# Attention heads: alternating score halves, one operand for the sample rows, merged mask and rotation operations

## The chip, the core and the metric

The kernel runs on one NeuronCore of a Trainium2 chip as a single program. The metric is its device time in microseconds (us); of several runs the median is taken. The core's engines run side by side and meet at semaphores: TensorE (PE, matmuls, with its weight loads shown as PEld), VectorE (DVE), ScalarE (ACT), GpSimd (POOL), and SyncE (SP), which issues DMA transfers. Each engine works through its own instruction list in the order in which it is written; an instruction that waits for a semaphore holds up what stands behind it on that engine.

## The reference, cut to what matters

One inference step of a two-layer decoder trunk: layer 0 is an mLSTM mixer, layer 1 a differential-attention mixer. There are 1024 prompt tokens (`SEQ`) and 8 sample sequences of 4 tokens, 32 sample rows in all (`TS`). The change touches the attention over the prompt, with 8 heads (`H_B`), two components c of 64 columns each per head, and values of 128 columns:

```
p = rmsnorm(x, g) @ w_kv
k = rope(p[..., :QK_B].reshape(bsz, t_, H_B, 2, DK_B), pos)
v = p[..., QK_B:].reshape(bsz, t_, H_B, DV_B)
...
s = jnp.einsum('bqhcd,bkhcd->bhcqk', q, kp).astype(F32) * ATTN_SCALE
s = jnp.where(mk, s, -jnp.inf)
p = jax.nn.softmax(jnp.concatenate(scores, axis=-1), axis=-1)
w = p[:, :, 0] - lam * p[:, :, 1]
o = jnp.einsum('bhqk,bkhe->bqhe', w, vp)
...
rope: concatenate([x1 * cos - x2 * sin, x2 * cos + x1 * sin])
```

So every query block of 128 tokens needs, for each component c, a score product against all earlier keys, a causal mask on its last 128 columns, a row maximum, an exponential and a row sum; the two exponentials are then combined with one coefficient per row and multiplied with V. The head outputs go through an RMSNorm, a SiLU gate and an output projection.

## The kernel before, in words

The program is a row of phases: input norm, gates, mLSTM for the prompt, mLSTM for the samples, an output stage, `attention_phase`, the paged decode attention of the samples, and a second output stage. Only `attention_phase` is changed (and the constant table that it reads; the decode phase reads its mask from a smaller table with another offset).

Float32 operands are split into a high part and a low part (names ending in H and L, such as XH and XL for the normed input, WH and WL for the weights), and a product is three matmuls: high by high, high by low, low by high. TensorE has 8 PSUM banks `BK[0]` to `BK[7]`. `BK[4]` to `BK[7]` are the tensors PD: two banks for the scores of component 0, two for component 1.

`heads` runs the 8 heads: `sweep1` of head 0, then a hardware loop over 7 heads with `sweep2(h)` followed by `sweep1(h + 1)`, then the last `sweep2` and a tail.

`sweep1` takes 9 blocks t of 128 tokens (t = 8, written t == NT, is the block of the 32 sample rows). TensorE projects Q and K (`project`, 8 contraction tiles by 3 products, 24 matmuls), VectorE applies the rotation (`rotate`, five operations, L1786 to L1799), TensorE transposes the result (L1969), and ScalarE and VectorE cut it into high and low parts QTH, KTH (L1684, L1685) and QTL, KTL (L1840, L1841). Between these, ScalarE and VectorE cut the next weights (L1639, L1764).

`sweep2` takes the query blocks t = 0 to 7. I call the time from the first score matmul of t to that of t + 1 step t. TensorE's order in step t is: `scores(h, t)` (L1914), `turn_weights(h, t - 1)` (transposes of the combined weights, L1925, into `BK[2]` and `BK[3]`), `project_values(t + 1)` (24 matmuls, L1899, into the single bank B_V), `turn_output(h, t - 2)` (L1945) and `weigh(h, t - 1)` (the product with V, L1937). `scores` issues component 0 completely and then component 1; component c contracts over partitions 64c to 64c + 63 (a 64-row operand). For t = 4 to 7 a component has six matmuls (two column chunks of at most 512), for t = 0 to 3 three.

VectorE's order in step t is, for component 0: mask (L1860), row maximum (L1862), scaling (L1863); for t > 4 the copy of the upper transposed weights out of `BK[3]` (`weights`, L1820); `output(h, t - 2)` (L1813, after GpSimd's root, L1725 to L1727); then mask, maximum and scaling for component 1; `o_transposed(h, t - 3)` (L1806), for which `turn_output` of the next block waits; `sigmoid` (L1848); the cut of the next head's weights (L1764); and then, after both exponentials, the coefficients (L1877 to L1879) and the combination of the two exponentials (L1880), for which `turn_weights` waits.

ScalarE's order in step t is: `values` (three reads of B_V, L1652 to L1654, which free it for the next `project_values`), `weights(h, t - 1)` (the copy of the lower transposed weights out of `BK[2]`, L1668), the two exponentials (L1702), two weight cuts (L1639) and `squares` (L1661).

## Time and profile before

| what | value |
|---|---|
| median of 3 runs | 2052.78 us (2051.82 to 2057.74) |
| the profiled execution | 2055.39 us |
| its span, first to last instruction | 2053.7 us |
| TensorE, weight loads busy | 1813.7 us, 1618.6 us |
| VectorE, ScalarE, GpSimd busy | 1150.5 us, 810.9 us, 378.3 us |
| mean granted TensorE clock | 0.928 of full speed |
| first matmul of the attention phase | 943.6 us after the span's start |

Busy time is the time in which an engine had an instruction of the program in it. Matmuls are pipelined: each record is longer than the distance to the next one, so start times say how fast TensorE goes. Idle time in front of an instruction is put down to what ended it.

### The profile page before, as it was taken

The page shows a single profiled execution, that of the slowest core. Times are in us where ns is not written, and L with a number is a line of the kernel's source. Part 1 is how long each engine was busy: PE and PEld are TensorE (multiplying, and loading weights), DVE is VectorE, ACT ScalarE, POOL GpSimd, SP SyncE. Part 2 cuts the span into 40 slices and gives each one's busy share as a digit, 9 for nine tenths or more (in the row PEclk, how much of TensorE's full clock was granted, in tenths as well). Part 3 has the DMA queues.
Part 4 walks back from the last instruction along what each step waited for, and adds up shares of the span by engine and source line. Part 5 has one row for each costly group of instructions (what it writes and reads, how often), then busy time and mean ns, then how long its engine had stood idle before and what let it go on. Part 6 is the DMA issues. An engine that isn't in the chain of part 4 may idle for free. (4 is left out here: it accounts for less than half of the span.)

```text
span 2053.7 us, 38516 instructions
## 1 busy us (share of the span) xinstructions
PE 1813.7 (88%) x12115; PEld 1618.6 (79%) x12115; DVE 1150.5 (56%) x3272; ACT 810.9 (39%) x2237; POOL 378.3 (18%) x823
## 2 busy tenths in 40 slices
PE   5399999999999687897999999999999778888698
PEld 4399999999999665687889898888989766666376
DVE  4443543543543444345767676676767556666553
ACT  5333333333333222233535444354443346665522
POOL 1021221221221212011213122131221201111101
PEclk8699999999999866898999999999999979898799
DMA  4213123113111023332121111211110067676532
GB/s 119 65 32 66 8 57 65 10 55 65 10 56 15 24 81 82 135 119 68 42 54 33 31 33 38 57 33 31 33 31 23 21 217 272 237 275 235 176 101 106
DMA packets 149133, 165.10 MB, mean 80 GB/s; under 512 B 12762, under 2 KB 118074, under 8 KB 149042
## 3 DMA queue, kind: packets, MB, share of 16 engines
q1 hardware_dynamic: 144738, 159.85, 26.2%
q0 software_dynamic: 1184, 4.23, 0.8%
q8 instruction: 32, 0.52, 0.1%
q10 hardware_dynamic: 3120, 0.01, 0.1%
q14 instruction: 59, 0.48, 0.1%
HBM read 138.69 MB, written 25.37 MB: 80 GB/s over the span
## 5 line engine op out<-in xcount | busy, mean ns | idle before, releaser
L809 PE MATMUL PS<-WH,XH 128*128 128x384 f32 (+3 forms) x1152 | 369.2, 320 | 2.1 <-DVE WORK L731 2.1
L809 PE MATMUL PS<-WL,XH 128*128 128x384 f32 (+3 forms) x1152 | 356.8, 310 | 0.0
L809 PE MATMUL PS<-WH,XL 128*128 128x384 f32 (+3 forms) x1152 | 356.4, 309 | 0.0
L809 PEld LDWEIGHTS PS<-WH,XH 128*128 128x128 f32 (+1 forms) x1152 | 207.9, 180 | 7.0 <-DVE WORK L731 2.6
L809 PEld LDWEIGHTS PS<-WL,XH 128*128 128x128 f32 (+1 forms) x1152 | 208.0, 181 | 4.1
L809 PEld LDWEIGHTS PS<-WH,XL 128*128 128x128 f32 (+1 forms) x1152 | 207.6, 180 | 4.6
L1899 PE MATMUL PS<-WH,XH 128*128 128x256 f32 (+1 forms) x576 | 173.3, 301 | 2.3 <-ACT WORK L1654 2.1
L1899 PE MATMUL PD<-WH,XH 128*128 128x256 f32 (+1 forms) x576 | 169.4, 294 | 2.8 <-PEq L142 2.8
L1899 PE MATMUL PS<-WL,XH 128*128 128x256 f32 (+1 forms) x576 | 167.0, 290 | 0.0
L1899 PE MATMUL PS<-WH,XL 128*128 128x256 f32 (+1 forms) x576 | 166.5, 289 | 0.0
L1899 PE MATMUL PD<-WL,XH 128*128 128x256 f32 (+1 forms) x576 | 163.9, 285 | 0.0
L1899 PE MATMUL PD<-WH,XL 128*128 128x256 f32 (+1 forms) x576 | 163.5, 284 | 0.0
L1702 ACT ACTIVATE WORK<-PD,WORK 128x256 f32<-128x256 f32 (+7 forms) x128 | 95.0, 742 | 80.6 <-DVE WORK L1863 79.9
L2326 PE MATMUL PS<-cst,RAW 128*128 128x128 f32 x512 | 86.2, 319 | 41.2 <-DVE XL L2233 35.6
L2326 PEld LDWEIGHTS PS<-cst,RAW 128*128 128x128 f32 x512 | 67.6, 163 | 59.2 <-DVE XL L2233 43.2
L1899 PEld LDWEIGHTS PS<-WH,XH 128*128 128x128 f32 (+1 forms) x576 | 108.5, 188 | 4.9 <-ACT WORK L1654 3.9
L1899 PEld LDWEIGHTS PS<-WH,XL 128*128 128x128 f32 (+1 forms) x576 | 108.6, 188 | 0.7
L1899 PEld LDWEIGHTS PS<-WL,XH 128*128 128x128 f32 (+1 forms) x576 | 108.4, 188 | 0.6
L1899 PEld LDWEIGHTS PD<-WH,XH 128*128 128x128 f32 (+1 forms) x576 | 105.3, 183 | 3.3 <-issue 2.9
L1899 PEld LDWEIGHTS PD<-WH,XL 128*128 128x128 f32 (+1 forms) x576 | 105.3, 183 | 0.5
L1899 PEld LDWEIGHTS PD<-WL,XH 128*128 128x128 f32 (+1 forms) x576 | 105.1, 182 | 0.5
L2233 DVE TENSOR_TENSOR XL<-PS,XH 128x512 fp32r<-128x512 f32 x128 | 83.9, 685 | 38.5 <-ACT XH L2154 38.3
(354 smaller groups left out, 4301.3 us busy)
## 6 DMA issues: line engine op xcount, KB each, us to landing
RAW<-in_cache_k SPq DMA_DIRECT2D x64, 512.0 KB, 4.6
WORK<-in_cache_v SPq DMA_DIRECT2D x64, 512.0 KB, 4.4
RAW<-in_w_in_a SPq DMA_DIRECT2D x40, 512.0 KB, 6.3
RAW<-in_w_in_b SPq DMA_DIRECT2D x16, 512.0 KB, 5.4
RAW<-in_w_kv SPq DMA_DIRECT2D x16, 512.0 KB, 5.4
out<-WORK SPq DMA_DIRECT2D x16, 512.0 KB, 3.1
WORK<-in_x_prompt SPq DMA_DIRECT2D x8, 512.0 KB, 4.4
WORK<-d_G SPq DMA_DIRECT2D x8, 512.0 KB
```

Of the source, the lines that this page charges most:

```text
L809: last = nc.tensor.matmul(bank[0:rows, 0:n], x[:, k, tt], reg(w)[:, k, :], start=(i == 0), stop=(i == 3 * KT - 1))
L1702: act.activation(PR[:, c, 0:(t + 1) * P], S[c][:, 0:(t + 1) * P], ACT.Exp, scale=ATTN_SCALE, bias=nm[:, c:c + 1], accum_out=sm[:, c:c + 1] ...
L1899: last = nc.tensor.matmul(bank[0:rows, 0:N], x[:, k, tt], reg(w, r)[:, k, :], start=(i == 0), stop=(i == 3 * KT - 1))
L2233: v.tensor_tensor(XL[cols], BK[j].rearrange("p (h t) -> p h t", h=4), XH[cols].bitcast(F32), ALU.subtract).then_inc(kl, 1)
L2326: x = nc.tensor.transpose(BK[j][:, h * P:(h + 1) * P], KB[:, p % 4, (4 * j + h) * P:(4 * j + h + 1) * P], ident)
```

## The change

There are five edits, all in `attention_phase`.

1. `scores` issues the matmuls of the two components alternately (c = 0, 1, 0, 1, ...), with one wait for both exponentials of the block before and one semaphore count at the end, where it had one wait and one count for each component.
2. `project_values(t + 1)` is split for t = 1 to 6: its first 12 matmuls now stand ahead of `turn_weights(h, t - 1)`, the other 12 behind it.
3. The 32 sample rows of XH and XL are laid side by side once into a 64-column operand XS, so that a sample projection takes 16 matmuls in place of 24. The halves of the result stand on partitions 0 to 31 and 32 to 63; ScalarE copies the upper half (`sample_low`) and VectorE adds it to the lower one.
4. VectorE masks both components with one operation over both pairs of banks, then does the two maxima; `output(h, t - 2)` moves behind the second maximum. One reciprocal of both row sums and a copy stand in the place of two reciprocals.
5. `rotate` has three operations of 256 columns in place of one of 256 and four of 128: the sine table holds its sign, and one operand is read with its 32-column halves swapped.

```
-C_MS = C_SIN + NB * HALF
+C_MS = C_SIN + NB * DK
...
-        c[:, C_SIN + t * HALF:C_SIN + (t + 1) * HALF] = np.sin(ang)
+        c[:, C_SIN + t * DK:C_SIN + t * DK + HALF] = -np.sin(ang)
+        c[:, C_SIN + t * DK + HALF:C_SIN + (t + 1) * DK] = np.sin(ang)
...
-        PD = [ctx.enter_context(nc.psum_tensor(f"PD{k}", [P, 2, 512], F32)) for k in range(2)]
+        PQ = ctx.enter_context(nc.psum_tensor("PD", [P, 4, 512], F32))
+        PD = [PQ[:, 0:2, :], PQ[:, 2:4, :]]
...
+            XS = phase_tensor("XS", [P, KT, 2 * TS], F32R)
...
+            SB = PQ[:, :, :].rearrange("p (c a) n -> p c (a n)", c=2)
+            SPARE = YX[:, KT * TOK:KT * TOK + 6 * P].rearrange("p (a c) -> p a c", a=6)
+            SM, TL = SPARE[:, 0:4, :], SPARE[:, 4:6, :]
...
+                    act.activation(XS[:, :, 0:TS], XH[:, :, SEQ:TOK].bitcast(F32), ACT.Copy)
+                    act.activation(XS[:, :, TS:2 * TS], XL[:, :, SEQ:TOK].bitcast(F32), ACT.Copy).then_inc(xs_set, 1)
                     act.wait_ge(lamS, 1)
                     act.activation(le, mx, ACT.Exp).then_inc(lamE, 1)
+                    def sample_low(bank, turn):
+                        act.wait_ge(smd, turn)
+                        act.activation(TL[0:TS, :, :], bank[TS:2 * TS, 0:N].rearrange("p (a c) -> p a c", a=2), ACT.Copy)\
+                           .then_inc(tlow, 1)
...
-                            act.activation(SM[0:TS, 2:4, :], B_V[0:TS, 0:2 * P].rearrange("p (a c) -> p a c", a=2),
-                                           ACT.Copy).then_inc(smd, 1)
+                            sample_low(B_V, 2 * h + 1)
...
+                            if t == NT:
+                                act.wait_ge(pj, 2 * NB * h + NB)
+                                sample_low(BK[4], 2 * h)
...
-                        src = BK[4 + t % 2][0:n, 0:N].rearrange("p (g c) -> p g c", c=HALF)
+                        src = BK[4 + t % 2][0:n, 0:N]
+                        if t == NT:
+                            dve.wait_ge(tlow, 2 * h + 1)
+                            links.link(v.tensor_tensor(TL[0:n, :, :], src.rearrange("p (a c) -> p a c", a=2),
+                                                       TL[0:n, :, :], ALU.add))
+                            src = TL[0:n, :, :].rearrange("p a c -> p (a c)")
                         cos = cst[0:n, C_COS + t * HALF:C_COS + (t + 1) * HALF]
-                        sin = cst[0:n, C_SIN + t * HALF:C_SIN + (t + 1) * HALF].unsqueeze(1).to_broadcast([n, 4, HALF])
-                        v.tensor_tensor(RA[0:n, :, :], src, cos.unsqueeze(1).to_broadcast([n, 8, HALF]), ALU.mult)
-                        v.tensor_tensor(RB[0:n, 0:8:2, :], src[:, 1:8:2, :], sin, ALU.mult)
-                        links.link(v.tensor_tensor(RB[0:n, 1:8:2, :], src[:, 0:8:2, :], sin, ALU.mult))
+                        sin = cst[0:n, C_SIN + t * DK:C_SIN + (t + 1) * DK].rearrange("p (a c) -> p a c", a=2)
+                        v.tensor_tensor(RA[0:n, :, :], src.rearrange("p (g c) -> p g c", c=HALF),
+                                        cos.unsqueeze(1).to_broadcast([n, 8, HALF]), ALU.mult)
+                        links.link(v.tensor_tensor(RB[0:n, :, :].rearrange("p (g a) c -> p g a c", a=2),
+                                                   src.rearrange("p (g a c) -> p g a c", a=2, c=HALF)[:, :, ::-1, :],
+                                                   sin.unsqueeze(1).to_broadcast([n, 4, 2, HALF]), ALU.mult))
                         if t < NT:
 
                             dve.wait_ge(tr[t % 2], 4 * h + t // 2)
                             dve.wait_ge(c_sst, 48 * h)
                             dst = SM[0:n, 0:2, :]
                         dst = dst.rearrange("p a (g c) -> p (a g) c", c=HALF)
-                        v.tensor_tensor(dst[:, 0:8:2, :], RA[0:n, 0:8:2, :], RB[0:n, 0:8:2, :], ALU.subtract)
-                        v.tensor_tensor(dst[:, 1:8:2, :], RA[0:n, 1:8:2, :], RB[0:n, 1:8:2, :], ALU.add)\
-                         .then_inc(rope, 1)
+                        v.tensor_tensor(dst, RA[0:n, :, :], RB[0:n, :, :], ALU.add).then_inc(rope, 1)
                         dve.wait_ge(rope, NB * h + t + 1)
+                        if t == NT:
+                            dve.sem_inc(smd, 1)
...
+                                dve.wait_ge(sc, NT * h + t + 1)
+                                links.link(v.tensor_tensor(SB[:, :, n - P:n], SB[:, :, n - P:n],
+                                                           cst[:, C_MB:C_MB + P].unsqueeze(1).to_broadcast([P, 2, P]),
+                                                           ALU.add))
                                 for c in range(2):
-                                    if c == 1 and t > 4:
-                                        weights(h, t - 1)
-                                    if c == 1 and t >= 2:
-                                        output(h, t - 2)
-                                    dve.wait_ge(sc, 2 * (NT * h + t) + c + 1)
-                                    links.link(v.tensor_tensor(S[c][:, n - P:n], S[c][:, n - P:n],
-                                                               cst[:, C_MB:C_MB + P], ALU.add))
                                     links.link(v.tensor_reduce(mx[:, c:c + 1], S[c][:, 0:n], AX, ALU.max, negate=True))
                                     v.tensor_scalar(nm[:, c:c + 1], mx[:, c:c + 1], ATTN_SCALE, None, ALU.mult)\
                                      .then_inc(mxs, 1)
+                                    if c == 0 and t > 4:
+                                        weights(h, t - 1)
+                                if t >= 2:
+                                    output(h, t - 2)
                             if t == NT:
                                 output(h, t - 2)
+                                dve.wait_ge(tlow, 2 * h + 2)
+                                v.tensor_tensor(SM[0:TS, 2:4, :], B_V[0:TS, 0:N].rearrange("p (a c) -> p a c", a=2),
+                                                TL[0:TS, :, :], ALU.add).then_inc(smd, 1)
...
-                                links.link(v.reciprocal(cf, sm[:, 1:2]))
-                                links.link(v.scalar_tensor_tensor(cf, sm[:, 0:1], nl, cf, ALU.mult, ALU.mult))
-                                v.reciprocal(rc[:, b:b + 1], sm[:, 0:1])
+                                links.link(v.reciprocal(rr1, sm))
+                                v.tensor_copy(rc[:, b:b + 1], rr1[:, 0:1])
+                                links.link(v.scalar_tensor_tensor(cf, sm[:, 0:1], nl, rr1[:, 1:2], ALU.mult, ALU.mult))
...
-                    def project(r, t, bank):
-                        rows = P if t < NT else TS
-                        tt = slice(t * P, t * P + rows)
-                        i = 0
+                    def project(r, t, bank, ks=range(KT)):
+                        tt = slice(t * P, t * P + P)
+                        for k in ks:
+                            for i, (x, w) in enumerate(((XH, WH), (XH, WL), (XL, WH))):
+                                last = nc.tensor.matmul(bank[:, 0:N], x[:, k, tt], reg(w, r)[:, k, :],
+                                                        start=(k == i == 0), stop=(k == KT - 1 and i == 2))
+                        if k == KT - 1:
+                            last.then_inc(pj, 1)
+                    def project_sample(r, bank):
                         for k in range(KT):
-                            for x, w in ((XH, WH), (XH, WL), (XL, WH)):
-                                last = nc.tensor.matmul(bank[0:rows, 0:N], x[:, k, tt], reg(w, r)[:, k, :],
-                                                        start=(i == 0), stop=(i == 3 * KT - 1))
-                                i += 1
+                            for w in (WH, WL):
+                                last = nc.tensor.matmul(bank[0:2 * TS, 0:N], XS[:, k, :], reg(w, r)[:, k, :],
+                                                        start=(k == 0 and w is WH), stop=(k == KT - 1 and w is WL))
                         last.then_inc(pj, 1)
+                    pe.wait_ge(xs_set, 1)
 
                     def scores(h, t):
                         width = (t // 2 + 1) * 2 * P
-                        for c in range(2):
-                            pe.wait_ge(ex, 2 * NT * h + max(2 * t - 1 + c, 0))
-                            rows = slice(DK * c, DK * c + DK)
-                            for at in range(0, width, 512):
-                                kk = slice(at, min(at + 512, width))
-                                i = 0
-                                for q, k in ((QTH, KTH), (QTH, KTL), (QTL, KTH)):
+                        pe.wait_ge(ex, 2 * (NT * h + t))
+                        for at in range(0, width, 512):
+                            kk = slice(at, min(at + 512, width))
+                            for i, (q, k) in enumerate(((QTH, KTH), (QTH, KTL), (QTL, KTH))):
+                                for c in range(2):
+                                    rows = slice(DK * c, DK * c + DK)
                                     x = nc.tensor.matmul(S[c][:, kk], q[rows, t * P:(t + 1) * P], k[rows, kk],
                                                          start=(i == 0), stop=(i == 2))
-                                    i += 1
-                            x.then_inc(sc, 1)
+                        x.then_inc(sc, 1)
...
+                            if t < NT:
+                                project(0, t, BK[4 + t % 2])
+                            else:
+                                project_sample(0, BK[4])
...
-                        def project_values(t):
-                            pe.wait_ge(vz, NT * h + t)
-                            pe.wait_ge(smd, h)
-                            project(1, t, B_V)
+                        def project_values(t, ks=range(KT)):
+                            if t == NT:
+                                pe.wait_ge(vz, NT * (h + 1))
+                                project_sample(1, B_V)
+                                return
+                            if 0 in ks:
+                                pe.wait_ge(vz, NT * h + t)
+                                pe.wait_ge(smd, 2 * h)
+                            project(1, t, B_V, ks)
...
+                            if t < NT - 1:
+                                project_values(t + 1, range(0, KT // 2))
                             turn_weights(h, t - 1)
-                            project_values(t + 1)
+                            if t < NT - 1:
+                                project_values(t + 1, range(KT // 2, KT))
+                            else:
+                                project_values(NT)
```

The next rows show the built program's TensorE list in step t = 5, in the loop over heads, before the change: the end of component 0's scores, component 1's scores, then the five transposes of `turn_weights(h, 4)` and the start of `project_values(6)`. PD are the score banks, PS the other banks.

```order
L1914 MATMUL PD<-WH,QTR 128x256
L1908 REGISTER_ALU
L1914 MATMUL PD<-WH,QTR 128x512
L1914 MATMUL PD<-WL,QTR 128x512
L1914 MATMUL PD<-WH,QTR 128x512
L1914 MATMUL PD<-WH,QTR 128x256
L1914 MATMUL PD<-WL,QTR 128x256
L1914 MATMUL PD<-WH,QTR 128x256
L1925 MATMUL PS<-cst,WORK 128x128 x4
L1923 REGISTER_ALU
L1925 MATMUL PS<-cst,WORK 128x128
L1975 REGISTER_ALU
```

The transposes follow the scores at once. The next rows show the same place of the changed program: all the scores of step 5 in pairs, and the start of the projection (its lines are now L1922).

```order
L1939 REGISTER_ALU
L1945 MATMUL PD<-WH,QTR 128x512 x2
L1945 MATMUL PD<-WL,QTR 128x512 x2
L1945 MATMUL PD<-WH,QTR 128x512 x2
L1945 MATMUL PD<-WH,QTR 128x256 x2
L1945 MATMUL PD<-WL,QTR 128x256 x2
L1945 MATMUL PD<-WH,QTR 128x256 x2
L2013 REGISTER_ALU
L1922 MATMUL PS<-WH,XH 128x256
```

Further on in the same step, where the first 12 projection matmuls end, the changed program has these rows.

```order
L1922 MATMUL PS<-WH,XL 128x256
L1955 MATMUL PS<-cst,WORK 128x128 x4
L1953 REGISTER_ALU
L1955 MATMUL PS<-cst,WORK 128x128
L1922 MATMUL PS<-WH,XH 128x256
```

The score rows are the same twelve matmuls in another order, and the five transposes have moved behind half of the projection.

On VectorE the list of step t = 4 was this before, from the mask of component 0 on.

```order
L1860 TENSOR_TENSOR PD<-PD,cst 128x128
L97 REGISTER_ALU
L1862 TENSOR_REDUCE WORK<-PD 128x1
L97 REGISTER_ALU
L1863 TENSOR_SCALAR WORK<-WORK 128x1
L1813 SCALAR_TENSOR_TENSOR WORK<-PS,WORK 128x128
L1859 REGISTER_ALU
L1860 TENSOR_TENSOR PD<-PD,cst 128x128
L97 REGISTER_ALU
L1862 TENSOR_REDUCE WORK<-PD 128x1
L97 REGISTER_ALU
L1863 TENSOR_SCALAR WORK<-WORK 128x1
```

The changed program has this list in the same place.

```order
L1876 TENSOR_TENSOR PD<-PD,cst 128x2x128
L94 REGISTER_ALU
L1880 TENSOR_REDUCE WORK<-PD 128x1
L94 REGISTER_ALU
L1881 TENSOR_SCALAR WORK<-WORK 128x1
L1880 TENSOR_REDUCE WORK<-PD 128x1
L94 REGISTER_ALU
L1881 TENSOR_SCALAR WORK<-WORK 128x1
L1834 SCALAR_TENSOR_TENSOR WORK<-PS,WORK 128x128
L1827 ISA
L1827 COPY YX<-PS 128x128
```

One mask operation is gone, and `output` (L1813, now L1834) has moved from between the two components to behind both.

## Rows read from the trace of the kernel before

**Rows 1.** The page: the span, and busy time of each engine.

```profile
span 2053.7 us, 38516 instructions
PE 1813.7 (88%) x12115; PEld 1618.6 (79%) x12115; DVE 1150.5 (56%) x3272; ACT 810.9 (39%) x2237; POOL 378.3 (18%) x823
```

**Rows 2.** Stretch of one head: us, each engine's busy time, clock, DMA.

```profile
1236.00:1322.00 86.00, 81.79 (x640) 75.98 (x640) 61.15 (x201) 38.16 (x129) 20.10 (x48) 0.98 0.14 39
```

**Rows 3.** Waits from 943 to 1636: total us, times, longest.

```profile
ACT WORK L1668 <- PE PS L1925: 83.5, 64, 2.0
...
DVE PD L1860 <- issue: 31.8, 6, 5.4
```

**Rows 4.** TensorE's timeline, scores of t = 3: start, us.

```profile
1253.79 0.51 PE L1914 MATMUL PD<-WH,QTR 64*128 64x512 f32 x2
...
1254.36 0.40 PE L1914 MATMUL PD<-WH,QTR 64*128 64x512 f32 x2
```

**Rows 5.** TensorE's timeline, scores of t = 5.

```profile
1265.56 0.50 PE L1914 MATMUL PD<-WH,QTR 64*128 64x512 f32 x1
...
1267.18 0.28 PE L1914 MATMUL PD<-WH,QTR 64*128 64x256 f32 x1
1267.39 0.77 PE L1925 MATMUL PS<-cst,WORK 128*128 128x128 f32 x5
```

**Rows 6.** ScalarE's timeline in step 5.

```profile
1268.08 0.60 ACT L1668 ACTIVATE WORK<-PS 128x512 f32<-128x512 f32 x1 [1.46 <-PE PS L1925]
1268.75 0.91 ACT L1702 ACTIVATE WORK<-PD,WORK 128x768 f32<-128x768 f32 x1
...
1270.64 0.90 ACT L1702 ACTIVATE WORK<-PD,WORK 128x768 f32<-128x768 f32 x1 [0.89 <-DVE WORK L1863]
1271.44 0.19 ACT L1702 ACTIVATION_READ_ACCUMULATOR WORK<-PD,WORK 128x1 f32 x1
```

**Rows 7.** VectorE's timeline in step 5.

```profile
1267.24 0.30 DVE L1860 TENSOR_TENSOR PD<-PD,cst 128x128 f32<-128x128 f32 x1
1267.57 0.96 DVE L1862 TENSOR_REDUCE WORK<-PD 128x1 f32<-128x768 f32 x1
...
1268.67 0.29 DVE L1820 COPY WORK<-PS 128x128 f32<-128x128 f32 x1
1268.88 0.34 DVE L1813 SCALAR_TENSOR_TENSOR WORK<-PS,WORK 128x128 f32<-128x128 f32 x1
...
1270.58 0.29 DVE L1806 COPY YX<-PS 128x128 f32 x1
```

**Rows 8.** TensorE's timeline, end of step 5.

```profile
1270.74 0.27 PE L1899 MATMUL PS<-WH,XL 128*128 128x256 f32 x1
1271.01 0.30 PE L1945 MATMUL PS<-cst,WORK 128*128 128x128 f32 x1
1271.34 1.35 PE L1937 MATMUL PS<-WORK 128*128 128x128 f32 x10
1272.62 0.49 PE L1914 MATMUL PD<-WH,QTR 64*128 64x512 f32 x1
```

**Rows 9.** All engines' timeline where a head's sweep2 begins.

```profile
1240.56 0.30 DVE L1860 TENSOR_TENSOR PD<-PD,cst 128x128 f32<-128x128 f32 x1 [5.40 <-issue]
...
1241.92 0.38 PE L1914 MATMUL PD<-WH,QTR 64*128 64x256 f32 x1 [1.76 <-ACT WORK L1702]
...
1243.42 0.28 ACT L1654 ACTIVATE WORK<-PS 128x128 f32<-128x128 f32 x1
...
1244.62 0.55 PE L1899 MATMUL PS<-WH,XH 128*128 128x256 f32 x1
```

**Rows 10.** A stretch behind it; the clock is the third number from the end.

```profile
1243.90:1247.30 3.40, 2.87 (x13) 2.88 (x14) 2.30 (x11) 1.76 (x7) 0.66 (x2) 0.50 0.00 0
```

**Rows 11.** Groups by form, 943 to 1636: count, busy us, mean ns.

```profile
L1786 DVE TENSOR_TENSOR WORK<-PD,cst 128x256 f32<-128x256 f32 x64 | 27.1, 424 | 25.4 <-PE PD L1899 25.3
...
L1899 PE MATMUL PS<-WH,XH 128*32 128x256 f32 x64 | 18.7, 291 | 0.0
```

**Rows 12.** DMA queues, one head: packets, MB, share.

```profile
q14 instruction: 5, 0.04, 0.2%
```

28 lines of the change are left out of this document (12 added, 16 removed).

## The prediction

> **What bounds the kernel now.** I read the page's list of engines first: TensorE is busy for 88% of the span, VectorE for 56%, ScalarE for 39% [rows 1]. The table by stretches shows the same in the stage that is changed: of a head's 86.00 us TensorE has 81.79 us with a matmul in it, VectorE 61.15 and ScalarE 38.16, at a clock of 0.98 [rows 2]. So TensorE is near its bound, yet not at it. The waits of this stage say where it meets the others: ScalarE waits 64 times, 83.5 us in all, for the transposed weights (L1925), and VectorE six times, 31.8 us in all, at the mask (L1860) with "issue" as the cause, where no work of another engine was late [rows 3]. So two chains matter: the ring transposes, ScalarE's copy, exponentials, combination, next transposes; and the stop at a head's beginning.
>
> Step t = 5 shows the ring. The scores start at 1265.56 and the last of their matmuls at 1267.18, 1.62 later, because component 1 follows component 0 [rows 5]. The transposes start at 1267.39. ScalarE waits 1.46 us for them, copies from 1268.08 on, and only then takes exponential 0 (1268.75), and exponential 1 at 1270.64, which waited 0.89 us for VectorE's scaling [rows 6]. VectorE's `o_transposed` begins at 1270.58 and takes 0.29 [rows 7]; `turn_output` starts just behind it (1271.01, ahead of it the last projection matmul at 1270.74), then `weigh` at 1271.34, and the next scores at 1272.62 [rows 8]. The step is 7.06 long, and of it TensorE idles only some tenths of a us. That is why little is to be had here without removing matmul time.
>
> **Edit 1, alternate scores.** At t = 3 the two components already run side by side: two matmuls start at 1253.79, the last two at 1254.36 [rows 4]. So for t = 0, 2, 3, where each has three matmuls, the edit changes nothing. From those rows, two paired steps of 512 columns take 0.57, so one takes 0.29 and one of 256 columns 0.14 (estimates). Twelve matmuls in pairs then have their last start 3 x 0.29 + 2 x 0.14 = 1.14 after the first, against 1.62 [rows 5]: 0.5 us is freed in each of the steps 4 to 7. Its bounds are 0 (something else ends the step) and 0.5.
>
> The edit also lets both components wait for both exponentials of the block before. Only at t = 1, where the scores wait 1.76 us for an exponential [rows 9], is this an exposed wait.
>
> **Edit 2, the split projection.** The 24 projection matmuls lie between the transposes (about 1267.9) and 1270.86, so half of them is 1.45 us. In steps 1 to 6 the transposes start that much later, less what edit 1 gives. In step 5: last score at 1.0 to 1.1 after the step's start, half projection to 2.75, transposes to 3.3, ScalarE's copy (0.60 [rows 6]) to 4.1, where it now ends at 3.12. Behind it wait exponential 0 (4.15 to 5.05, before 3.19 to 4.1) and exponential 1 (5.05 to 6.05; before 5.08 to 5.98). VectorE's copy of the upper bank (L1820) also waits for the transposes, to about 3.8, and behind it stand maximum 1 (0.96), `output` and `o_transposed`. With VectorE's savings `o_transposed` runs from 5.15 to 5.45 where it was 5.02 to 5.31 [rows 7], and `turn_output` and `weigh` follow: the step ends at about 7.15, +0.1. So the split eats the 0.5 of edit 1 in step 5. I take the same +0.1 for t = 6, and for t = 4, where VectorE copies nothing, -0.2. For t = 2 and 3 edit 1 gives nothing to pay with and I take +0.2 each. Bounds of each of these steps: -0.5 (the later transposes are covered by ScalarE's 1.46 of waiting [rows 6]: it is already idle there) and +0.9 (the whole remaining delay 1.45 - 0.5 reaches the end). I stay near the lower end because the second half of the projection now stands where TensorE would wait.
>
> Step 7 isn't split, so edit 1's 0.5 counts there; -0.3 is left, since VectorE's mask, which now needs both components, and its chain of 0.96 maxima [rows 7] end the step rather than TensorE.
>
> At t = 0 and 1 TensorE is idle. The scores of t = 1 start at 1241.92 after 1.76 of waiting, `values` is done at 1243.70, but `project_values(2)` starts only at 1244.62, because it stands behind `turn_weights(0)`, which waits for the combination [rows 9]. With the first half ahead of the transposes it can begin some 0.15 after `values`. Less the joint wait of edit 1, 0.6 to 0.7 becomes 0.5: -0.5. Bounds 0 and -0.9.
>
> **Edit 3, samples.** Two projections a head go from 24 to 16 matmuls. A projection matmul starts every 2.9 / 24 = 0.12 us, so each saves 0.95. A sample matmul's record is 291 ns long [rows 11], longer than that distance, which leaves the cadence at 0.12. The one in `sweep1` is TensorE's time; the one at t = 8 stands in step 7, whose end VectorE sets, and I count nothing. New beside it are a ScalarE copy of some 0.4 and a VectorE add of some 0.4 (by the 424 ns of a 256-column operation [rows 11]), under the transposes of other blocks. If that cover fails it costs 0.8 a head. The two copies for XS are about 1 us once, at the start of the phase.
>
> **Edits 4 and 5.** The merged mask takes about 0.42 (that row again) in place of 2 x 0.30 [rows 7], 0.2 off VectorE in each step, already used in step 5 above. The rotation gives VectorE some 0.15 a block in `sweep1`, where VectorE waits 25.3 us for TensorE's projections [rows 11], so it is worth nothing. If reading from two banks or with swapped halves is slow (bound: 0.85, two such operations), the mask costs 0.2 a step instead.
>
> **Sum.** Per head -0.5 (t = 0, 1), +0.4 (2, 3), -0.2 (4), +0.2 (5, 6), -0.3 (7), -0.95 (samples): -1.35, by 8 heads -10.8, plus 1 at the start: -9.8. The profiled execution of 2055.4 becomes 2045.6, and the median, 2.6 below it, 2043.0.
>
> **Rivals.** A: this, 2034 to 2050 (0 to -18.8 by the bounds that are near).
> B: the split hides wholly. ScalarE's 1.46 of waiting [rows 6] speaks for it, the order copy before exponential against it. Then steps 4 to 7 give 0.5 each, 2 and 3 nothing: -0.5 - 2.0 - 0.95 = -3.45 a head, -27.6 + 1: 2026.
> C, the other side: the transposes' delay pushes the exponentials, and so the combination for which the next transposes wait, round the ring. One step alone would not do it; it decides from about 0.35 us lost net in each of the steps 2 to 6. With 0.45 in each, 2.25 a head stand against the -0.5, -0.3 and -0.95 of the other terms: +0.5, +4 in all. To that comes the clock. It is at 0.50 for 3.40 us behind the stop at the head's start [rows 10], which costs 1.7 us of full speed; a longer wait in a step could bring such a stretch in some more heads, three of them +5. With the 1 at the start that is 2053 + 10 = 2063.
> D: the stop at the head's start goes. VectorE starts its mask at 1240.56 after 5.40 without any instruction, right behind the loop's branch [rows 9], six times 5.3 us [rows 3]; in a head five packets with 0.04 MB of instructions are fetched on its queue [rows 12]. VectorE's loop body shrinks from 352 to 324 instructions, 8%, which hardly changes what must be fetched, so I expect the stop to stay. If it went, the scores of t = 1 could start when the projection before them ends, at about 1239.0 and not 1241.92, and the slow stretch would go in part: 2.9 + 1.15, six times, -24: 2019.
> The Trainium skill ("Runtime: NRT & Kernel Launch", Instruction fetch mechanics) says that an engine holds two pages of 256 instructions and stalls on a taken branch whose target lies outside them. By that rule a body of 324 can lie in two pages where 352 can't, depending on where it starts, and the time would be D's. The packets of [rows 12] are 8 KB each and not the 16 KiB of that section, which weakens it.
> E: nothing nets out: t = 0, 1 gains nothing, or the sample's chain is exposed. 2050 to 2054, say 2051.
>
> **Chances.** A 0.5, B 0.12, C 0.15, D 0.07, E 0.16. A measurement of this kernel tells 0.3%, 6 us, from no change: 2046.6 to 2058.9. Of A's 0.5 I put 0.11 above 2046.6. Faster: 0.39 + 0.12 + 0.07 = 0.58; same: 0.11 + 0.16 = 0.27; slower: 0.15. The range runs from 2024, which takes in B and leaves out D, to 2058, which leaves out C and little else.
>
> **What would show it.** Right: scores of t = 5 start in pairs with the last start near 1.1; the transposes near 2.8; ScalarE's copy near 3.5, exponential 0 at 4.15; `o_transposed` at 5.15; a step 5 of 7.1 to 7.2; `project_values(2)` about 0.6 earlier in the head; `sweep1` shorter by 0.95; "issue" before the mask still 5.3, six times; one slow stretch a head. Wrong: steps 2 to 4 longer by more than 0.35, steps 4 to 6 shorter by 0.5, the stop at the loop gone, a merged mask above 0.6, or more time at half clock.

## The result and the profile after

The changed kernel takes 2059.88 us (median of 20 runs, 2052.85 to 2064.0), the kernel before 2052.96 us (20 runs): a ratio of 1.003, 95% interval 1.002 to 1.004. It is slightly slower; I had forecast 2043. The profiled execution took 2057.89 us.

The page of the changed kernel, its span and busy times (against [rows 1]):

```profile
span 2056.2 us, 37932 instructions
PE 1789.1 (87%) x11987; PEld 1594.7 (78%) x11987; DVE 1134.1 (55%) x3080; ACT 806.4 (39%) x2247; POOL 372.8 (18%) x823
```

TensorE has 24.6 us less to do, VectorE 16.4, and the span is 2.5 us longer. So the work was removed and waiting took its place. The same head as in [rows 2], in the view by stretches:

```profile
1234.00:1320.60 86.60, 78.64 (x622) 72.89 (x624) 59.05 (x177) 37.41 (x130) 18.82 (x48) 0.96 0.14 38
```

The waits of the changed kernel from 943 to 1636 say which:

```profile
ACT WORK L1678 <- PE PS L1955: 140.7, 64, 3.2
...
DVE PD L1876 <- issue: 39.0, 6, 6.6
...
PE PS L1975 <- DVE YX L1827: 25.4, 25, 1.6
PEld PD L1945 <- ACT WORK L1715: 24.7, 6, 4.2
...
PE PD L1945 <- ACT WORK L1715: 23.5, 6, 4.0
```

ScalarE's wait for the transposed weights (L1678, 64 times) grew from 83.5 to 140.7 us, and the stop at the mask of t = 0 (L1876, six times) from 31.8 to 39.0 us [rows 3]. TensorE waits 23.5 us for the exponentials of t = 0 before it can issue the scores of t = 1 (L1945), and 25.4 us at `turn_output` (L1975) for `o_transposed`. In the kernel before these two waits were short:

```profile
PE PD L1914 <- ACT WORK L1702: 9.9, 6, 1.8
...
PE PS L1945 <- DVE YX L1806: 5.3, 10, 2.5
```

From the starts of the first score matmuls, the mean length of each step over the six heads 1 to 6 (us; the last column but one runs from the scores of t = 7 through `sweep1` to the next head):

```
kernel                      t=0   t=1   t=2   t=3   t=4   t=5   t=6   7+sweep1  head
before                      5.73  7.69  4.74  5.51  6.27  7.05  7.72  41.48    86.19
after                       7.97  5.85  4.95  5.49  6.01  7.14  8.05  41.48    86.94
before, alternation         6.35  6.51  4.72  5.51  6.21  7.14  7.70  41.47    85.61
before, split               5.60  6.19  5.01  5.98  6.35  8.10  9.01  41.47    87.70
before, 51 increments       4.00  4.05  4.82  5.54  6.27  7.05  7.71  41.46    80.90
after, 64 increments        3.99  4.15  4.95  5.48  6.02  7.25  8.04  41.75    81.62
  and unsplit               3.99  4.05  4.73  5.24  5.71  6.84  7.46  40.98    79.01
  unsplit, two masks        3.98  4.04  4.80  5.48  5.93  7.09  7.66  42.22    81.20
  unsplit, serial scores    3.98  4.05  4.73  5.27  6.28  7.20  8.04  41.53    81.06
```

The lower rows are the experiments below. Between the first two rows, t = 0 and 1 together lose 0.40, t = 2 loses 0.21, t = 4 wins 0.26, t = 5 loses 0.09 and t = 6 loses 0.33. The last part is even on the mean, but only because it takes some 40.75 in three heads, 0.73 less than before, and 42.0 to 42.3 in the three others. In these three TensorE runs at half clock for 3.4 us where step 7 ends and `sweep1` begins. The first of the next rows is the wait at `turn_output` in step 7 of head 4, the second the stretch behind it (the clock is the third number from the end):

```profile
1371.63 0.30 PE L1975 MATMUL PS<-cst,WORK 128*128 128x128 f32 x1 [1.57 <-DVE YX L1827]
...
1373.00:1376.40 3.40, 3.40 (x19) 3.40 (x18) 1.99 (x6) 1.42 (x5) 0.93 (x3) 0.50 0.01 2
```

**Step 5** of the changed kernel, scores from 1264.51, all engines' timeline (against [rows 5 to 8]):

```profile
1265.55 0.28 PE L1945 MATMUL PD<-WH,QTR 64*128 64x256 f32 x2
...
1267.32 0.71 PE L1955 MATMUL PS<-cst,WORK 128*128 128x128 f32 x5
1267.96 0.60 ACT L1678 ACTIVATE WORK<-PS 128x512 f32<-128x512 f32 x1 [2.38 <-PE PS L1955]
...
1268.45 0.90 ACT L1715 ACTIVATE WORK<-PD,WORK 128x768 f32<-128x768 f32 x1
...
1269.63 0.28 DVE L1827 COPY YX<-PS 128x128 f32 x1
...
1270.06 0.30 PE L1975 MATMUL PS<-cst,WORK 128*128 128x128 f32 x1 [0.58 <-DVE YX L1827]
...
1271.67 0.50 PE L1945 MATMUL PD<-WH,QTR 64*128 64x512 f32 x2
```

Relative to the first score: last score 1.04, transposes 2.81, ScalarE's copy 3.45, exponential 0 at 3.94, `o_transposed` 5.12, next scores 7.16. The working had 1.0 to 1.1, 2.75, 3.5, 4.15, 5.15 and 7.15. This step is about as forecast, with exponential 0 0.2 earlier; the loss sits elsewhere.

**The head's beginning** in the changed kernel, head 3 (scores of t = 0 at 1233.89; against [rows 9]):

```profile
1240.06 0.43 DVE L1876 TENSOR_TENSOR PD<-PD,cst 128x256 f32<-128x256 f32 x1 [6.59 <-issue]
1241.94 0.29 PEld L1945 LDWEIGHTS PD<-WH,QTR 64*128 64x128 f32 x2 [4.20 <-ACT WORK L1715]
1241.94 0.58 PE L1945 MATMUL PD<-WH,QTR 64*128 64x256 f32 x2 [4.00 <-ACT WORK L1715]
```

The mask now starts 6.17 us after the head's first score; before it was 4.47. Of the 1.70 the stop itself is 1.19 (6.59 against 5.40); 0.51 is that VectorE's last operation of `sweep1` ends closer to that score (0.42 ahead of it, before 0.93), since the sample rotation now waits for ScalarE's copy and an add. Run 10 below, without these two, has 0.95 again, where run 6 with them has 0.46. The scores of t = 1 come 8.05 after those of t = 0, where it was 5.83.

### The profile page after: what moved, and what is told of

Same layout as the page of the kernel before. It is cut to its first block and busy times, and to the rows that moved or that the text cites. A ratio compares the mean times of both kernels' runs of the same rounds, so it can differ in the third digit from the quotient of the medians.

```text
span 2056.2 us, 37932 instructions
## 1 busy us (share of the span) xinstructions
PE 1789.1 (87%) x11987; PEld 1594.7 (78%) x11987; DVE 1134.1 (55%) x3080; ACT 806.4 (39%) x2247; POOL 372.8 (18%) x823
## 5 line engine op out<-in xcount | busy, mean ns | idle before, releaser
L807 PEld LDWEIGHTS PS<-WH,XH 128*128 128x128 f32 (+1 forms) x1152 | 208.1, 181 | 7.0 <-DVE WORK L729 2.6
L807 PEld LDWEIGHTS PS<-WL,XH 128*128 128x128 f32 (+1 forms) x1152 | 208.5, 181 | 4.0
L807 PEld LDWEIGHTS PS<-WH,XL 128*128 128x128 f32 (+1 forms) x1152 | 207.7, 180 | 4.6
L1922 PE MATMUL PS<-WH,XH 128*128 128x256 f32 x512 | 159.1, 311 | 7.5 <-ACT WORK L1665 6.4
L1922 PE MATMUL PD<-WH,XH 128*128 128x256 f32 x512 | 151.7, 296 | 3.3 <-ACT XS L1646 3.3
L1922 PE MATMUL PS<-WL,XH 128*128 128x256 f32 x512 | 147.9, 289 | 0.0
L1922 PE MATMUL PS<-WH,XL 128*128 128x256 f32 x512 | 147.6, 288 | 0.0
L1922 PE MATMUL PD<-WL,XH 128*128 128x256 f32 x512 | 146.5, 286 | 0.0
L1922 PE MATMUL PD<-WH,XL 128*128 128x256 f32 x512 | 145.9, 285 | 0.0
L1922 PEld LDWEIGHTS PS<-WH,XH 128*128 128x128 f32 x512 | 100.5, 196 | 24.9 <-ACT WORK L1665 17.3
L1922 PEld LDWEIGHTS PD<-WH,XH 128*128 128x128 f32 x512 | 99.0, 193 | 3.4 <-ACT XS L1646 3.4
L1922 PEld LDWEIGHTS PS<-WL,XH 128*128 128x128 f32 x512 | 100.6, 196 | 0.0
L1922 PEld LDWEIGHTS PS<-WH,XL 128*128 128x128 f32 x512 | 100.5, 196 | 0.0
L1922 PEld LDWEIGHTS PD<-WL,XH 128*128 128x128 f32 x512 | 99.0, 193 | 0.0
L1922 PEld LDWEIGHTS PD<-WH,XL 128*128 128x128 f32 x512 | 98.8, 193 | 0.0
```

Of the source, the lines that this page charges most:

```text
L807: last = nc.tensor.matmul(bank[0:rows, 0:n], x[:, k, tt], reg(w)[:, k, :], start=(i == 0), stop=(i == 3 * KT - 1))
L1922: last = nc.tensor.matmul(bank[:, 0:N], x[:, k, tt], reg(w, r)[:, k, :], start=(k == i == 0), stop=(k == KT - 1 and i == 2))
```

## The experiments

Two theories stand behind the first runs. Theory S: the split of the projection costs as much as the other edits give. Theory L: VectorE's stop at the loop's start, longer by 1.2 us, is the loss. Ratios are to the kernel before, run on the same chip; its median was 2052.6 us for the first four runs, 2049.58 for the next four, 2056.66 for the third set and 2050.76 for the last two, so ratios are compared and not medians. Where two of my kernels are compared that did not run in the same set, the quotient of their ratios is taken.

**1. The split taken back.** In `sweep2` of the changed kernel:

```
-                            if t < NT - 1:
-                                project_values(t + 1, range(0, KT // 2))
                             turn_weights(h, t - 1)
-                            if t < NT - 1:
-                                project_values(t + 1, range(KT // 2, KT))
-                            else:
-                                project_values(NT)
+                            project_values(t + 1)
```

> The changed kernel with project_values(t + 1) in one piece again, behind turn_weights; all else as changed. Theory S (the split costs what the alternation gives): the steps 2 to 6 shrink, t = 2 by 0.2 and t = 5 and 6 by 0.4 to 0.5 each, ScalarE's wait for the transposes falls from 140.7 back to about 85 us, TensorE's wait at turn_output from 28 to under 10: some -2 us a head, 2044 us. Theory L (VectorE's stop at the loop's start, now 6.5 us in place of 5.3, and what stands behind it, is all of the loss): the steps 2 to 6 hardly change, 2058 us.

Measured 2048.25 us, 0.9978 (0.9964 to 0.9992). ScalarE's wait for the transposes fell to 65.1 us. Steps 2 to 6 sum to 29.89 against 31.64, -1.75 a head, so the split does cost; but t = 0 and 1 took 15.39 in place of 13.82. TensorE's clock goes with most of that: behind the stop, half-clock stretches lost 3.4 us in each of the six heads, where they lost 1.7 in four and 3.4 in two of the changed kernel's, 1.1 a head of the 1.57. The rest goes with `project_values(2)`, which without the split starts 0.9 later in the head (9.9 us after the first score, with it 9.05). The 2044 us expected for theory S were not reached.

**2. The split alone**, put into the kernel before (the same lines the other way).

> The kernel before with the split alone. Theory S: without alternation nothing pays for the later transposes: each of the steps 2 to 6 grows by 0.2 to 0.6, +1.5 to +2.5 a head, less some 0.5 at t = 1: 2063 to 2068 us. Theory L: the split is free, 2049 to 2053 us.

Measured 2068.92 us, 1.008 (1.0068 to 1.0093). Steps 3, 5 and 6 grew by 0.47, 1.05 and 1.29, the last two more than expected; t = 0 and 1 together took 11.79 in place of 13.42, with `project_values(2)` 1.0 earlier in the head. Theory S holds for its part.

**3 and 4. VectorE's loop moved within its list.** N increments of a semaphore that nobody reads stand at the start of VectorE's part of the attention phase, 64 in the changed kernel and 51 in the kernel before:

```
                     links = Chain(dve, dch)
+                    for _ in range(64):
+                        dve.sem_inc(pads, 1)
```

Measured 2023.19 us, 0.9856 (0.984 to 0.9872). That is a little more than I expected. The 6.5 us stop is gone: at the head's beginning VectorE waits 1.08 us for TensorE, and the scores of t = 1 come 4.0 us after those of t = 0.

```profile
1223.29 0.39 PE L1948 MATMUL PD<-WH,QTR 64*128 64x256 f32 x2
...
1223.95 0.43 DVE L1879 TENSOR_TENSOR PD<-PD,cst 128x256 f32<-128x256 f32 x1 [1.08 <-PE PD L1948]
...
1227.29 0.38 PE L1948 MATMUL PD<-WH,QTR 64*128 64x256 f32 x2
```

> The kernel before with 51 such increments at the same place; its body of 352 instructions then touches three pieces of 128 as well. Theory L: the 5.3 us stop goes, TensorE's 1.76 us of waiting at t = 1 goes and with it the stretch at half clock: -2.9 to -4 us a head, six times, 2029 to 2036 us. Rival: 2053 us, stop 5.3 us.

Measured 2021.7 us, 0.9854 (0.9836 to 0.9873), with no "issue" wait at the mask left and, from 980 to 1590, not one half-clock stretch. With the stop out of both, changed kernel and kernel before are equal within the noise: 0.9856 and 0.9854.

**5. Alternation alone** in the kernel before; each component's last matmul still counts `sc`.

```
+                        pe.wait_ge(ex, 2 * (NT * h + t))
                         for at in range(0, width, 512):
+                            for i, (q, k) in enumerate(((QTH, KTH), (QTH, KTL), (QTL, KTH))):
+                                for c in range(2):
```

> The kernel before with alternate scores alone (one joint wait for both exponentials; each component's last matmul still counts the semaphore, so VectorE's order is unchanged). Theory S (alternation is worth its 0.5 us in steps 4 to 7 as long as the transposes stay right behind the scores): steps 4 to 7 -0.4 to -0.5 each, t = 1 +0.1: -1.6 a head, 2040 us. Rival C (the clock takes it back: more half-speed stretches, as the run with the unsplit projection had 34.3 us lost against 27.3): 2047 to 2053 us.

Measured 2051.97 us, 1.001 (1.0 to 1.002). Both expectations were wrong on the reason: steps 3 to 6 are as long as before (within 0.1), with no clock needed to take anything back. The head of this trace is 0.58 shorter, all of it at t = 0 and 1, where this execution lost 1.7 us to half clock in each head, and the kernel before 3.4 in two of the six and 1.7 in the others. Step 5's end in this kernel (scores from 1261.65):

```profile
1265.62 0.96 DVE L1862 TENSOR_REDUCE WORK<-PD 128x1 f32<-128x768 f32 x1
1266.74 0.29 DVE L1806 COPY YX<-PS 128x128 f32 x1
1267.14 0.14 PEld L1943 LDWEIGHTS PS<-cst,WORK 128*128 128x128 f32 x1 [0.42 <-issue]
1267.17 0.30 PE L1943 MATMUL PS<-cst,WORK 128*128 128x128 f32 x1 [0.24 <-DVE YX L1806]
```

`o_transposed` starts 5.09 after the first score, 5.02 before. TensorE is done earlier and waits for it (16.0 us in the stage at this place, 5.3 before). So in step 5 VectorE's chain of masks and maxima ends the step, and not TensorE's matmuls.

**6 and 7. The split taken back and 64 increments**, then also `output(h, t - 2)` back between the components.

> The changed kernel with the projection in one piece and the 64 increments. If the split's price (11.6 us) and the stop's (36.7 us) add up: 2052.6 + 6.9 - 11.6 - 36.7 = 2011 us; if the split's price was masked in the first run by longer half-clock stretches after the stop (34.3 us lost against 30.8), it is larger: -2.0 to -2.5 a head, 2004 to 2007 us. Rival (they share what they save): 2016 to 2021 us.

Measured 2004.0 us, 0.9782 (0.9765 to 0.9799): the fastest kernel of the study. Against run 3 it is 0.75% faster, 15 us: the split's price with the stop gone. Steps 2 to 6 give 1.76 us a head of it and t = 1 gives 0.10, 15 us in eight heads; in the profiled executions three half-clock stretches fewer come on top.

> As the run before, and VectorE's output(h, t - 2) stands between the two components again, behind the first scaling and the copy of the weights, as in the kernel before; the merged mask stays. Theory M (with output behind the second maximum, o_transposed and so turn_output come late at t = 6 and 7, where TensorE waits 19 us in all and 22.7 in its weight loads): the waits at turn_output fall under 10 us, -0.5 to -1 a head, 4 to 8 us faster than the run before. Rival (exponential 1 gets later by the same 0.35 us and the step is as long): no change.

Measured 2007.74 us, 0.9793 (0.9778 to 0.9807): no change that can be told. The wait at `turn_output` stayed (19.3 and 19.4 us). That fits the rival: where `output` stands in VectorE's chain doesn't alter its sum.

**8 and 9. Controls for the increments**: 128 and 16 in place of 64.

> The changed kernel with 128 increments in place of 64: control for the third run. If pieces of 128 instructions decide, the loop's body lies to them as without any increments: the stop of 6.5 us is back and the time is 2058 to 2062 us. Rival (any shift, or the increments themselves, did it): 2023 us.

> The changed kernel with 16 increments: its loop body starts at the same place of VectorE's list as in the kernel before (931) and still touches four pieces of 128 instructions. If the start's place sets how long the stop is, it falls from 6.5 to 5.3 us, the first instruction fetch behind the branch comes at about 3.3 us instead of 1.2 and 4.8, and the time is 2053 us. If the shorter body sets it, 6.5 us stay and the time is 2060 us.

128: 2062.24 us, 1.0058 (1.0042 to 1.0075), the stop is back. 16: 2052.0 us, 0.9984 (0.997 to 0.9999), the stop is nearly that of the kernel before (5.5 against 5.3). Run 8 has the stop of the changed kernel and a ratio 0.28% above it, with a head that is not longer (86.43 against 86.94); so ratios of such kernels agree to some 0.3% only. The waits at the mask of t = 0, first with 128, then with 16:

```profile
DVE PD L1879 <- issue: 39.5, 6, 6.7
```

```profile
DVE PD L1879 <- issue: 33.0, 6, 5.8
```

The trace has the instruction fetches on VectorE's queue (q14, packets of 8192 bytes). VectorE starts one instruction right behind the loop's branch and then stops; it goes on at +5.8 in head 3 of the kernel before, at +7.0 in the changed one. In the first 8 us behind the branch packets start at:

```
before            +3.3 to 3.6   +6.0 to 6.6
after             +1.2 to 1.5   +4.7 to 4.9   +7.3 to 7.5
after, 16         +3.5 to 4.0   +6.2 to 6.7
after, 128        +1.1 to 1.5   +4.7 to 5.0   +7.3 to 7.6
after, 64         none, and none in the rest of the loop
```

In every turn VectorE goes on 2.1 to 2.3 us after the start of one of these packets: the one at +3.3 to 4.0 where there are two, the one at +4.7 to 5.0 where there are three. Stop and packets come and go together, so the stop is a wait for instructions.

**10 to 12. Parts of the best kernel undone**: the sample rows by 24 matmuls, the components' scores one after the other, and a mask operation for each component. In run 10 the two copies that fill XS stayed in, other than its expectation says; that is 0.5 us once.

> The best kernel so far (the changed one, projection in one piece, 64 increments) with the sample rows projected by 24 matmuls as in the kernel before: no operand XS, no copy and no add. If the 16-matmul form is worth its matmuls in sweep1 (0.95 a head), the time is 2004 + 7.6 = 2012 us; if copy and add eat it, 2004 us; if they cost more, 2000 us.

> The best kernel so far with component 0's scores issued completely before component 1's, still one wait and one count. If alternation is what shortened steps 3 to 6 (5.54, 6.27, 7.05, 7.71 to 5.24, 5.71, 6.84, 7.46), steps 4 to 7 grow by 0.5 each, since the merged mask waits for the last matmul: 2004 + 16 = 2020 us. If VectorE's chain ends these steps, part of it: 2008 to 2012 us.

> The best kernel so far with one mask operation for each component again (0.30 each in place of 0.43), output left behind the second maximum. If VectorE's chain sets o_transposed and with it the step, steps 4 to 6 grow by 0.1 to 0.2 each: +4 us, 2008 us. If the merged mask is worth nothing, 2004 us.

```
-                                links.link(v.tensor_tensor(SB[:, :, n - P:n], SB[:, :, n - P:n],
...
+                                    links.link(v.tensor_tensor(S[c][:, n - P:n], S[c][:, n - P:n],
+                                                               cst[:, C_MB:C_MB + P], ALU.add))
```

Samples: 2010.84 us, 0.9781 (0.9757 to 0.9804) against 0.9782: worth nothing that can be told. In the traces `sweep1` and step 7 take 41.2 without the 16-matmul form and 40.8 with it, where no half-clock stretch falls into them: 0.4 a head, some 3 us, which is less than these intervals. Serial scores: 2025.67 us, 0.9856 (0.9833 to 0.9879), with steps 4 to 6 longer by 0.57, 0.36 and 0.58. Two masks: 2026.27 us, 0.9846 (0.9823 to 0.9868), with steps 3 to 6 each 0.20 to 0.25 longer and five half-clock stretches from 980 to 1570, near the start of `sweep1`, where run 6 has one. Undoing either costs 0.65% to 0.75%: alternation pays only together with the shorter mask. With serial scores the merged mask also waits for the last matmul of both components, so run 11 prices the pair's order under this mask and not alternation by itself. Run 12 has edits 1, 3 and 5 and the rest of edit 4 without the merged mask and is at 0.9846, where the kernel before without its stop is at 0.9854: together these give nothing that can be told. Edit 5 was not tried by itself.

**13 and 14. How the late transposes reach the step's end**, both with the split and 64 increments.

> The changed kernel with 64 increments, the split kept, and ScalarE's copy of the transposed weights moved from before exponential 0 to between the two exponentials; exponential 0 still waits until the transposes have read PR, which it overwrites. Theory K (the split costs time because the copy of 0.3 to 0.6 us stands between the late transposes and exponential 0): step 6 loses most of its 0.6 against the unsplit kernel, -0.3 in each of the steps 2 to 6, 2011 to 2014 us on the scale on which the split and the unsplit kernel with 64 increments have 2023 and 2004. Theory R (the read of PR itself is the binding wait, or VectorE's copy and o_transposed behind it are): under 0.1 a step, 2019 to 2024 us.

> The changed kernel with 64 increments, the split kept, and VectorE's output(h, t - 2) between the two components, as in the kernel before. Theory O (output behind the second maximum makes turn_output late at t = 6 and 7, and that idle TensorE time is what brings the half-clock stretches near the start of sweep1): the stretches of 3.4 us near there, four in this stage's loop, go, step 6 -0.3: 2013 to 2017 us. Rival (VectorE's chain has the same sum either way, as with the unsplit projection): 2021 to 2025 us.

```
+                                if t >= 1:
+                                    act.wait_ge(wt[0], NT * h + t)
...
+                                    if c == 1 and t >= 1:
+                                        weights(h, t - 1)
                                     act.wait_ge(mxs, 2 * (NT * h + t) + c + 1)
```

13: 2023.54 us, 0.9874 (0.9853 to 0.9895). 14: 2027.65 us, 0.989 (0.9871 to 0.991). Step 6 is 8.04 and 8.09, as with neither. So neither ScalarE's copy nor `output`'s place carries the delay. Run 13's trace has no half-clock stretch from 980 to 1590 where run 3's has four, at the same step 6; run 14 has five. By its median run 13 is no faster than run 3, while its profiled execution, at 2020.17 us, is the fastest of its four. The stretches vary among kernels with the same wait, and I can't forecast them. Step 6 of run 3 (split, scores from 1255.15):

```profile
1258.27 0.82 PE L1958 MATMUL PS<-cst,WORK 128*128 128x128 f32 x6
1258.45 0.15 DVE L1884 TENSOR_SCALAR WORK<-WORK 128x1 f32<-128x1 f32 x1
...
1259.13 0.42 DVE L1844 COPY WORK<-PS 128x256 f32<-128x256 f32 x1 [0.52 <-PE PS L1958]
...
1259.47 1.08 DVE L1883 TENSOR_REDUCE WORK<-PD 128x1 f32<-128x896 f32 x1
...
1261.36 0.30 PE L1978 MATMUL PS<-cst,WORK 128*128 128x128 f32 x1 [0.84 <-DVE YX L1830]
```

And of run 6 (unsplit, scores from 1247.65):

```profile
1249.25 0.88 PE L1958 MATMUL PS<-cst,WORK 128*128 128x128 f32 x6
...
1251.05 0.42 DVE L1844 COPY WORK<-PS 128x256 f32<-128x256 f32 x1
...
1251.39 1.08 DVE L1883 TENSOR_REDUCE WORK<-PD 128x1 f32<-128x896 f32 x1
...
1253.29 0.30 PE L1978 MATMUL PS<-cst,WORK 128*128 128x128 f32 x1 [0.32 <-DVE YX L1830]
```

Unsplit, the transposes are there when VectorE has scaled component 0, and its copy doesn't wait. Split, the copy waits 0.52 us, and everything behind it, the second maximum and `o_transposed`, comes 0.58 later (copy at 3.98 and 3.40 after the first score). That is the size of step 6's difference, 8.04 to 7.46. Putting `weights` behind the second maximum wasn't tried.

## Why the prediction was wrong, point by point

By the table of steps, the forecast and the measurement per head, in us:

```
                    forecast   measured
t = 0 and 1         -0.5       +0.40
t = 2 and 3         +0.4       +0.19
t = 4               -0.2       -0.26
t = 5 and 6         +0.2       +0.42
step 7 and sweep1   -1.25       0.00   (-0.73 in the three heads without the half-clock stretch there)
head                -1.35      +0.75
```

- **Step 5** and its working were right (+0.1 forecast, +0.09 measured), **t = 2** (+0.2, +0.21) and **t = 4** (-0.2, -0.26) too; t = 3 was forecast at +0.2 and came out at -0.02. **t = 6** was mis-sized: "the same +0.1" measured +0.33. The maxima grow with the block, and the copy that waits for the transposes stands in front of the longer of them. Over steps 2 to 6 the sum is right: +0.4 forecast, +0.35 measured.
- **The first failed step is t = 0 and 1**, with -0.5 a head, and in it the sentence that the stop "stays". I treated it as a constant with one alternative, that it vanishes. It depends on where the loop's body lies in VectorE's list, and the edits moved its start by 16 places, from 931 to 915. It grew by 1.2 us, the 0.5 us of later sample rotation, which I had put under other work, came to it, and t = 0 and 1 lose 0.40. `project_values(2)` starts 0.6 later in the head and not 0.6 earlier. Undoing only that shift (run 9) takes 1.003 to 0.9984. By these two ratios the move costs about 0.5%, 9 us (run 8 against run 9, the same two stops on one chip, gives 0.7%), so without it the kernel would have been within 0.3% of the kernel before: still not my forecast, but on the border of cases A and E. In run 9 t = 0 and 1 take 12.94, 0.48 less than before, and `project_values(2)` starts 0.4 earlier though the mask starts 0.7 later: there the split does what I forecast. But run 9 also lost 0.6 us a head less to half clock than the kernel before, so how much of the 0.48 is the split's stays open.
- **The second failed step is step 7 and `sweep1`**, -0.3 and -0.95. It is the largest miss of the sum. In the heads without a half-clock stretch there, step 7 gave 0.2 and `sweep1` 0.5; in the three others the stretch took it all back.
- **Edit 1** was priced by TensorE: 0.5 us in steps 4 to 7. Alone it gives nothing in steps 3 to 6 (run 5). I had read TensorE's 81.79 busy us of 86.00 [rows 2] as a bound with tenths of slack, while `o_transposed` ended just ahead of `turn_output` [rows 7, 8]: the two engines were tied, and relieving one gives nothing.
- **Edit 4** is the opposite: I wrote its 0.2 us off as used up. It lets alternation pay; together they give 0.2 to 0.6 us in each of the steps 3 to 6, 1.4 a head over steps 2 to 6 (run 6 against run 4). That is the 1.5 that I had given to edit 1 for steps 4 to 6: the size was right and the reason was not.
- **Edit 2** eats what edits 1 and 4 give, as forecast in kind. Its price was right too. My working holds 1.9 us a head for steps 2 to 6, as the difference to edit 1 alone (0.2, 0.2, 0.3, 0.6 and 0.6); run 3 against run 6 has 1.76 (0.22, 0.24, 0.31, 0.41 and 0.58). With the 0.10 at t = 1 that is 15 us. What it should have bought at t = 0 and 1 is nothing once the stop is gone (t = 1 takes 4.15 with it and 4.05 without). By run 6 against run 4, 0.9782 to 0.9854, the edits without the split are worth -0.7%, 15 us; with it nothing.
- **Samples**: the working had -0.95 in `sweep1` and nothing at t = 8. In head 3 `sweep1` became shorter by 0.50 (from 33.30 to 32.80), since the next projection, which stood 0.14 behind the last transposes, now stands 0.52 behind them. VectorE's last weight cut (L1777) ends just ahead of it; that it is the cause is argued from the order of the rows, not shown by a run. At t = 8 nothing, as written: TensorE waits 1.6 us for `o_transposed` in step 7.
- **Clock**: I expected one slow stretch a head. There is a second one in three of six heads, from the end of step 7 into `sweep1`, behind TensorE's 1.6 us of waiting; it costs some 1.5 us each by the table, 4.4 us in the profiled execution. Rival C had just this, three more stretches for +5 behind a longer wait, though not its other condition of 0.35 us lost in each of the steps 2 to 6 (measured 0.07). The stretches are the part of the loss whose cause stays open: runs 8, 9 and 13 have the same 1.6 us wait in all of the heads 1 to 6 and no such stretch in any of them.
- **Rival D's** mechanism was real, but not its place: the stop can be removed and it is worth 1.5% (31 us in the kernel before), the largest single item found. I gave it 0.07, since the smaller body seemed to change little; what counts is how many pieces the body touches. The page I named ("Runtime: NRT & Kernel Launch" of the Trainium skill, Instruction fetch mechanics) has the mechanism right, a taken branch to code that isn't held waits for a fetch. Its two pages of 256 instructions would have had room for the 324 of the changed kernel, places 915 to 1238, two such pages counted from the list's start, yet the stop grew; and run 3's body, 979 to 1302, touches three and doesn't stop. Counting the pages from another place doesn't help: run 3 has no stop at 979 and run 8, only 64 places on, has it back, and no border of pages of 256 puts the bodies at 915 and at 1043 into three pages and the one at 979 into two. Here the measurement decides: the packets are of 8 KB, 128 instructions if that section's 16 KiB hold 256.

## What to carry to other kernels

An engine that is 88% busy may still be tied with a chain on another one. Before pricing matmul time that is saved, look whether the wait at the end of the step would merely grow, and change both engines together. A wait put down to "issue" behind a loop's branch (5.3 to 6.6 us here) is worth a look at the instruction fetch packets first. If there are fetches in every turn, shifting the loop by some dozens of cheap instructions may remove it, and any edit that changes the count ahead of the loop may move it by chance; so compare kernels with the stop taken out of both. And moving half of a projection ahead of something that two engines wait for is not free filling, even where both show waits there.

## What was not expected of the hardware

- The same 3.4 us stretches at half clock (1.2 GHz) that follow the stop also follow a wait of 1.6 us in TensorE's list, but not each time: in three of the heads 1 to 6 of the changed kernel, in none of them in runs 8, 9 and 13. With the stop gone from the kernel before, none was left between 980 and 1590.
